# Turning the squares of the hidden tiles: sixteen VectorE transposes, or one and sixteen SBUF transfers

## The reference

```
def swiglu(x, w_gu, w_down):
    g, u = jnp.split(x @ w_gu, 2, axis=-1)
    return (jax.nn.silu(g) * u) @ w_down
...
    for l in range(DEPTH):
        f = swiglu(rms_norm(x, ffn1_pre_g[l]), ffn1_w_gu[l], ffn1_w_down[l])
        x = x + 0.5 * rms_norm(f, ffn1_post_g[l])
        m = hybrid_mixer(rms_norm(x, mix_pre_g[l]), mix_w_in[l], mix_w_out[l],
        ...
        x = x + rms_norm(m, mix_post_g[l])
        f = swiglu(rms_norm(x, ffn2_pre_g[l]), ffn2_w_gu[l], ffn2_w_down[l])
        x = x + 0.5 * rms_norm(f, ffn2_post_g[l])
```

## Time and profile before

| | us |
|---|---|
| Median of 3 runs | 1882.7 (1882.63 to 1883.42) |
| The profiled execution | 1883.3 |
| its span, first to last instruction | 1882.0 |
| TensorE busy | 1873.4 |
| VectorE busy | 1574.0 |
| ScalarE busy | 1103.4 |
| GpSimd busy | 153.5 |
| 1280 transposes of L1994 | 387.4 |

### The profile page before, as it was taken

How to read it: one execution, slowest core, us unless ns; L and a number is a source line. 1 busy time by engine, 2 the same in 40 slices (tenths; PEclk the granted TensorE clock), 3 DMA queues, 4 the chain that set the end, 5 groups by cost and what they waited for, 6 DMA issues and landing times.

```text
span 1882.0 us, 25018 instructions
## 1 busy us (share of the span) xinstructions
PE 1873.4 (100%) x8974; PEld 1572.4 (84%) x8974; DVE 1574.0 (84%) x3072; ACT 1103.4 (59%) x1812; POOL 153.5 (8%) x193
## 2 busy tenths in 40 slices
PE   9999999999999999999999999999999999999999
PEld 7888998888888898888888888888888888888887
DVE  7998789988898868998799878689879987858986
ACT  6554876555655586655555557555555555656553
POOL 1120030000000013000000014100000000500000
PEclk9999999999999999999999999999999999999999
DMA  6765535665666553665466645356655664535653
GB/s 247 238 220 180 197 128 188 217 199 168 199 229 213 168 191 124 201 205 198 160 214 213 204 144 186 113 182 201 201 165 192 212 202 152 180 113 193 206 193 111
DMA packets 97787, 350.25 MB, mean 186 GB/s; under 512 B 10880, under 2 KB 12032, under 8 KB 97408
## 3 DMA queue, kind: packets, MB, share of 16 engines
q1 hardware_dynamic: 95184, 340.13, 54.6%
q10 hardware_dynamic: 2448, 8.53, 1.3%
q0 software_dynamic: 32, 0.00, 0.0%
HBM read 347.57 MB, written 1.05 MB: 185 GB/s over the span
## 4 chain that ended last, share of the span: by engine, by line
PE 94%; DVE 3%; ACT 1%; issue 1%; DMA 0%; SPq 0%; POOL 0%; DVEq 0%; ACTq 0%
PE ps_gu L482 18%; PE ps_gu L480 18%; PE ps_gu L481 18%; PE ps_acc L480 10%; PE ps_acc L482 10%; PE ps_acc L481 10%; PE ps_gu L726 1%; PE ps_gu L727 1%; PE ps_gu L728 1%; PE ps_acc L500 1%; DVE sb_wl L1932 1%; PE ps_gu L1074 0%; DMA sb_scratch<-stream 0%; PE ps_acc L1035 0%; PE ps_tr L480 0%
## 5 line engine op out<-in xcount | busy, mean ns | idle before, releaser
L480 PE MATMUL ps_gu<-sb_wh,sb_xh 128*128 128x512 f32 (+2 forms) x1592 | 620.4, 390 | 0.3 <-DVE sb_wl L1929 0.3
L482 PE MATMUL ps_gu<-sb_wh,sb_xl 128*128 128x512 f32 (+2 forms) x1592 | 617.2, 388 | 0.0
L481 PE MATMUL ps_gu<-sb_wl,sb_xh 128*128 128x512 f32 (+2 forms) x1592 | 616.7, 387 | 0.0
L1257 ACT ACTIVATE sb_wh<-sb_raw,sb_const 128x512 fp32r<-128x512 f32 x344 | 248.2, 721 | 274.6 <-DMA sb_raw<-stream 130.2
L1994 DVE STREAM_TRANSPOSE sb_scratch<-sb_scratch 32x128 f32<-32x128 f32 x1280 | 387.4, 303 | 24.8
L1932 DVE TENSOR_TENSOR sb_wl<-sb_raw,sb_wh 128x1024 fp32r<-128x1024 f32 (+2 forms) x296 | 352.5, 1223 | 23.2 <-ACT sb_wh L1261 20.7
L482 PEld LDWEIGHTS ps_gu<-sb_wh,sb_xl 128*128 128x128 f32 x1592 | 298.9, 188 | 60.0
L480 PEld LDWEIGHTS ps_gu<-sb_wh,sb_xh 128*128 128x128 f32 x1592 | 299.0, 188 | 59.7 <-issue 1.3
L481 PEld LDWEIGHTS ps_gu<-sb_wl,sb_xh 128*128 128x128 f32 x1592 | 299.1, 188 | 58.6
L1261 ACT ACTIVATE sb_wh<-sb_raw 128x1024 fp32r<-128x1024 f32 (+2 forms) x296 | 302.4, 1044 | 64.7 <-DMA sb_raw<-stream 29.6
L1927 DVE SCALAR_TENSOR_TENSOR sb_wl<-sb_raw,sb_const,sb_wh 128x512 fp32r<-128x512 f32 x344 | 257.6, 749 | 90.4 <-ACT sb_wh L1258 90.1
(11 more groups left out here) (279 smaller groups left out, 1580.2 us busy)
## 6 DMA issues: line engine op xcount, KB each, us to landing
sb_raw<-stream SPq DMA_DIRECT2D x620, 512.0 KB, 4.4
sb_raw<-stream SPq DMA_DIRECT2D x8, 416.0 KB, 4.1
sb_raw<-stream SPq DMA_DIRECT2D x8, 390.0 KB, 3.7
sb_scratch<-stream SPq DMA_DIRECT2D x6, 512.0 KB, 8.6
sb_gpost<-post_gains ACTq DMA_DIRECT2D x6, 512.0 KB, 5.2
sb_params<-params ACTq DMA_DIRECT2D x2, 1128.5 KB, 7.7
sb_scratch<-gain_rows ACTq DMA_DIRECT2D x4, 512.0 KB, 5.9
sb_raw<-stream SPq DMA_DIRECT2D x4, 384.0 KB, 3.1
```

Of the source, the lines that this page charges most:

```text
L480: pe.matmul(out, xh, wh, start=start, stop=False)
L481: pe.matmul(out, xh, wl, start=False, stop=False)
L482: return pe.matmul(out, xl, wh, start=False, stop=stop)
L1257: go(m.wh[:, u % RING, 0:512], m.unit(u)[:, 0:512], ACT.Copy, scale=m.gpre[:, e, k:k + 1])
```

## The change

`turn_squares` becomes one VectorE transpose of all 128 partitions x 512 columns (sixteen squares in each quarter of the partitions). It turns every square but leaves it on its own quarter of the partitions, in a new buffer `m.squares`. The squares are then moved to their quarter by sixteen SBUF-to-SBUF transfers of 32 partitions x 128 floats (16 KB) each, into `m.hid_t`, whose layout is now by source quarter. SP issues the eight from quarters 0 and 1, ScalarE's queue the eight from quarters 2 and 3; a semaphore counts 256 for the sixteen. `both_high` waits for this count. SP's step stands ahead of the load of the fourth unit behind the transpose's place (`moves`), ScalarE's between the two units of down weights of the chunk (for the first chunk of a stage, behind them both). Both wait for the transpose, and for `both_low` of the chunk before, since `m.hid_t` is overwritten. The transpose waits for the moves of the chunk before, since `m.squares` is overwritten. `both_high` and `both_low` work on the same values in another order, with runs of 32 elements.

More of the change, by code:

```diff
@@ L236, in __init__ @@
         self.squared = Signal(nc, "hidden_squares_turned")
+        self.moved = [nc.alloc_semaphore(f"hidden_squares_moved_{k}") for k in two]
         self.both_high = Signal(nc, "hidden_high_both")
@@ L439, in both_places, with quarter, by_square @@
     return slice(2 * (j % 2), 2 * (j % 2) + 2)
-def square(a, of_partitions, of_columns):
-    blocks = a.rearrange("p t (i n) -> p (t i) n", i=2)
-    return blocks[32 * of_partitions:32 * of_partitions + 32, :, 32 * of_columns:32 * of_columns + 32]
+def quarter(i):
+    return slice(32 * i, 32 * i + 32)
+def turn_after_split(f, j):
+    return FIRST_UNIT[FFN_STAGE[f]] + 8 + 6 * j
+def by_square(a):
+    return a.rearrange("p t (c i n) -> p (t c) i n", c=2, i=4)
 def by_head(a, n):
@@ L1999, in both_low @@
         places = both_places(j)
-        tt(m.hl[:, places, :], m.hid_t, m.hh[:, places, :].bitcast(F32), ALU.subtract).then_inc(*s.both_low.up())
+        tt(by_square(m.hl[:, places, :]), m.turned_hid, by_square(m.hh[:, places, :]).bitcast(F32), ALU.subtract).then_inc(
+            *s.both_low.up())
     def last_low(f, t):
@@ L2928, in load_second, with move_squares @@
         sp.dma_start(m.unit(1)[:, cols], aps["stream"][1, :, cols]).then_inc(s.loaded(1)[0], 16)
+    def move_squares(f, j):
+        n = squared_count(f, j)
+        sp.wait_ge(*s.squared.at(n))
+        if n > 1:
+            sp.wait_ge(*s.both_low.at(n - 1))
+        for i in range(2):
+            for to in range(4):
+                sp.dma_start(m.hid_t[quarter(to), i], m.squares[quarter(i), to]).then_inc(s.moved[n % 2], 16)
+    moves = {turn_after_split(f, j) + RAW: (f, j) for f in range(len(FFN_STAGE)) for j in range(LAST)}
     load_x(0, 0)
@@ L2946, in sync_program @@
         load(u)
+    move_squares(LAST_FFN, LAST - 1)
     n = 0
```

2 lines of the change are left out of this document (1 added, 1 removed).

## The result

The changed kernel takes 1899.8 us (median of 4 runs, 1898.1 to 1902.8) against 1882.9 us for the kernel before on the same chip: a ratio of 1.0091, 95% interval 1.0074 to 1.0109. It is slower by 17 us, where I had forecast 1882.4 and a range up to 1890. Its profiled execution took 1898.1 us, with a span of 1896.8.

The account below looks back on a forecast made before the run. TensorE was taken as the bound, busy 1873.4 of 1882.0 us; the terms summed to -0.3 us at the first hand-over and 0 elsewhere, from a median of 1882.7 to 1882.4 us, range 1881 to 1890.

Parts of the forecast that it names:

- The bound, and that VectorE's relief is worth nothing: Whole kernel: TensorE, busy 1873.4 of 1882.0 us, sets the time; freeing VectorE of 348 us shortens nothing directly.
- Step 1: VectorE: one 128x512 transpose of 0.70 us replaces sixteen taking 5.05 us; upper bound 1.21 us.
- Step 3: Landing of the moves: 2.2 us after issue, upper end 4.4; the last lands 6.38 us after the zero.
- Step 4: both_high and both_low behind the landing: 32-element runs cost nothing; first chunk's both_low ends at 7.8 us, against 8.1.
- Step 6: SP's queue: eight issues ahead of one weight load, which goes 4.65 us after the zero instead of 6.4; no cost.
- Step 2: Both issuing queues: eight issues at 0.475 us each, upper end 0.64, the last starting 4.18 us after the zero.
- step 5: ScalarE's queue stands 3.8 us; in middle chunks both_low ends at 8.3 us against 9.5, last turned chunk about 8.3.
- The round of 12.4 us: ScalarE's work from zero to zero, under TensorE's 16.3 and VectorE's present 15.15, so room grows faster after a late start.
- The moves land late: Rival at each stage's first chunk: landing of 4.4 us makes TensorE wait; 1888 to 1902 us, put at 1893, chance 0.15.
- the upper end of the issues: Issue price of 0.64 us instead of 0.475 on each queue, 1.2 us more; with late landing 1898 us.
- the third rival: In every chunk, each queue's small transfers are paid one behind the other, 2.2 us each; about 2500 us, chance 0.02.

Follow-up runs that it names:

- none: The changed kernel with all sixteen transfers left out, both engines reading the unmoved squares; 1882.0 us, 0.9985 to 1.0004 of the kernel before.
- diag12: The changed kernel with the four squares that keep their partitions turned in place by VectorE, six transfers per queue; 1884.3 us.
- dram: The changed kernel with SP writing the squares to DRAM in one transfer and fetching them in four, ScalarE issuing none; 1928.1 us.
- sp8: The changed kernel with only SP's eight transfers, ScalarE's eight left out and unmoved squares read; 1883.3 us.
- pool8: The changed kernel with ScalarE's eight transfers sent by GpSimd in stages 2 to 7; 1900.2 us.

## Why the prediction was wrong

- *The bound, and that VectorE's relief is worth nothing* stood: TensorE has the same 8974 matmuls at the same pitch, and `none` is at 0.9994.
- *Step 1* stood: 80 transpositions of 711 ns (0.70 forecast; four times the small form, 1.21 us, was not paid), VectorE at 1239.6 us ("near 1230"). *Step 3* stood in size: 2.4 us to landing as the median of all moves against 2.2, and 1.8 us for the last move of a first chunk. *Step 4*: reads in runs of 32 elements cost nothing (both_high 620 ns, L2030 687 ns). *Step 6* was off by the issues too, but harmless: SP's load goes 5.8 us after the zero, not at 4.65, and still ahead of the 6.4 us of before. ScalarE's busy time is 1075.0 us, where I had "near 1103".
- *Step 2 failed: the term of the issues was too small*, and the loss hangs on it (with 4.0 us of issues, in diag12, all but 1.2 of the 17 us are gone). Eight issues take 5.3 us on ScalarE and not 3.8 (SP 5.0), and the last starts 5.6 us after the zero and not 4.2. I had two prices, 0.475 us from two issues in a row and 0.64 from six, and took the lower, explaining the higher by "much queued ahead". The number of issues in a row doesn't tell the two apart either. In the kernel before nine more issues of SP end where the six of the earlier trace rows begin:

```profile
1.16 0.90 SPq L463 DMA_DIRECT2D sb_scratch<-stream  x2
2.10 1.39 SPq L2923 DMA_DIRECT2D sb_x<-x  x3
3.53 0.91 SPq L2928 DMA_DIRECT2D sb_scratch<-stream  x2
4.48 0.91 SPq L2923 DMA_DIRECT2D sb_x<-x  x2
```

They stand 0.47 to 0.48 us apart, so nine in a row ran at the lower price; of the five distances in the six one is 0.48 and four are 0.66 to 0.70. In dram four fetches of 64 KB and the two loads behind them are 0.47 apart again:

```profile
313.96 1.75 SPq L2968 DMA_DIRECT2D sb_scratch<-squares  x4
315.75 0.91 SPq L2948 DMA_DIRECT2D sb_raw<-stream  x2
```

The moves from SBUF to SBUF were 0.63 or 0.64 apart in every run, four, six, eight or sixteen in a row. Loads from DRAM were seen at both prices (those behind SP's moves in sp8 stand 0.62 us apart in the median), so neither the count nor the direction of the transfer explains the price; what sets it no run shows. The kernel before has no move from SBUF to SBUF in its rows, so they gave a range for the price and no choice in it.
- *What the issues did in the first chunk*: the last starts 1.4 us late and its landing is 0.4 us shorter than forecast, which makes 8.8 against 7.8. But 0.64 us alone would not have given the time. Put into my sum it is `both_low` at 9.0 us in first chunks, which is late in the first stage alone (TensorE comes at 7.9 there and at 9.1 in the next tightest): an estimate of some 1883.5 us from the rows of before. The rest is step 5 and the places.
- *Step 5 failed twice.* It has the longer standing again (+1.5 us), and it let `both_low` follow `both_high` directly. VectorE's own order has the low parts of two units ahead of it, and these can't start before ScalarE's unit behind the issues. In the second chunk shown above `both_high` ends at 1455.56 and `both_low` starts at 1456.41. diag12 agrees: its issues last 4.00 us, near the 3.8 of my forecast, and `both_low` still ends 9.3 us after the zero in middle chunks, not 8.3. So of the 2.3 us that the forecast was off, 1.5 are issues and 0.8 is VectorE's queue. The round of 12.4 us, from ScalarE's work alone, was wrong for the same reason: issues until 6.2 us after the zero, 1.1 until L1276's result, 8.0 of VectorE's work make 15.3. So the room didn't grow faster after a late start, as I wrote; it grows by 1.0 us a chunk.
- *The places.* I worked out first, middle and last turned chunks, with the third chunk standing for the middle ones. The second, which has the least room (1.2 us in the median, 0.06 in the first stage) and inherits the first's delay, was not looked at. It is the largest item, 5.6 of 11.9 us. For the last turned chunk I had "about 8.3"; it ends at 10.3 in the median, where 1.8 us of room had been, and loses 3.4 us.
- *The rivals.* "The moves land late" came nearest in size: its price with the upper end of the issues is 1898. That is luck. It has 15 us at first chunks, where the run lost 1.4, its cause, a landing of 4.4 us, isn't what happened, and it looked for no stall behind the first chunk. I gave it 0.15 and put it at 1893, the middle of its two lower prices. The 2.0 us that the third rival takes from the Trainium skill (page "DMA: Bandwidth & Descriptors", section "Anatomy of one DMA") are stated there for transfers that GpSimd issues. These moves went by SP and ScalarE; they landed 2.4 us after their issue in the median, and the next went 0.63 us behind, so they were not paid one behind the other.
- *What wasn't in it at all*: long issues. 17 of ScalarE's 640 issues and 12 of SP's take 0.95 to 2.2 us in place of 0.6 (the second of ScalarE's rows 0.87). One falls in a last turned chunk (zero 1095.38):

```profile
1096.22 6.35 ACTq L1325 DMA_DIRECT2D sb_scratch<-sb_scratch  x8
...
1106.79 0.50 PE L495 MATMUL ps_acc<-sb_wh,sb_fr 128*128 128x512 f32 x1 [0.19 <-DVE sb_fr L2030]
```

The packet of an instruction queue in the stretch of that chunk from 1098 to 1102 us (packets, MB, share):

```profile
q8 instruction: 1, 0.02, 1.4%
```

Such an issue adds a us to a chunk that has little left: without one, `both_low` of a last turned chunk ends at 10.27 us and TensorE comes at 10.4 to 11.05. Of the four large stalls at last turned chunks three (0.4, 0.6 and 0.8 us) have one in the chunk itself. The largest, 1.6 us in the first stage, has none there; it is inherited. Three rounds of that stage take 17.0, 17.7 and 16.9 us in place of 15.3, so its ninth chunk has 1.2 us of room, where the other stages have 3.0 to 4.5. The last two of the three have long issues; in the first ScalarE waits for weights that land late, probably beside a load of 1128.5 KB that it had sent itself 7.6 us before:

```profile
101.73 0.73 ACT L1272 ACTIVATE sb_wh<-sb_raw,sb_const 128x512 fp32r<-128x512 f32 x1 [2.02 <-DMA sb_raw<-stream]
```

All 29 long issues have a packet of an instruction queue within 2 us before their start or 0.5 us after their end, as has one in five of the other issues. Over ten kernels of the table (all but before, none, pool8 and dram) it is 206 of 209 long issues (0.9 us and more) and 1820 of 8623 others. That fetching instructions holds the issue up is a likely reading; no run here takes the fetches away, so it stays open.

## What to carry over

Where the rows have two prices for a DMA issue and none for the kind of transfer that the change makes, carry both through the sum, at every place; the number of issues in a row did not pick the right one here. Count an issue as standing time of the engine that issues, with the landing on top where that engine waits next. Then follow each engine's own order up to the hand-over, since a consumer further back in the queue of another engine gains nothing from data that are there early. The room to look for is that of the tightest place with what it inherits from the place before: an added delay costs nothing up to it and its full length beyond.
